# Row sums merged per head, squares as two bf16 terms, modulation as rows, and a first stage by half tiles in a hybrid attention and convolution layer on Trainium2

## The reference

```python
shift, scale, gate = jnp.split(mod, 3, axis=-1)          # mod = c @ w_ada + b_ada
u = layer_norm(x) * (1.0 + scale[:, None]) + shift[:, None]
proj = jnp.einsum('bsd,de->bse', u, w_in)
q, k, v, z_a, bg, cg, xin, z_c = jnp.split(proj, IN_SPLITS, axis=-1)
...
s = s + bias[None, :, None]                              # causal, T5 bias, 8 heads, 2 maps of 64
p = jax.nn.softmax(s, axis=-1)
a = p[:, :, 0] - lam * p[:, :, 1]                        # differential map, then a @ v
...
o = o * lax.rsqrt(jnp.mean(jnp.square(o), axis=-1, keepdims=True) + RMS_EPS)
y_attn = o * subln_gain * (1.0 - lambda_init) * jax.nn.silu(z_a)
y_conv = short_conv(bg, cg, xin, conv_w) * jax.nn.silu(z_c)
merged = g_a * (y_attn @ w_branch[0]) + g_c * (y_conv @ w_branch[1])
out = jnp.einsum('bsd,de->bse', merged, w_out)
return layer_norm(DEEPNORM_ALPHA * x + (1.0 + gate[:, None]) * out, ln_gain, ln_bias)
```

## Time and profile before

| | us |
|---|---|
| median of 3 runs (lowest, highest) | 3925.77 (3921.51, 4459.56) |
| the profiled execution, all cores | 3949.52 |
| span of its slowest core (core 1) | 3948.0 |
| spans of the cores | 3879.9 to 3948.0 |
| mean granted TensorE clock of the cores | 0.974 to 0.984 |

### The profile page before, as it was taken

One profiled execution on the slowest core, in us unless ns is written; L12 is line 12 of the kernel. 1 busy time (PEld: TensorE's weight loads), 2 busy tenths in 40 slices (PEclk: granted clock), 3 DMA queues, 4 the chain that ended last, 5 costly groups with the idle time before them and its releaser, 6 DMA issues.

```text
span 3948.0 us, 69802 instructions; the slowest of 8 cores (3879.9 to 3948.0 us)
## 1 busy us (share of the span) xinstructions
PE 3688.0 (93%) x18936; PEld 1530.1 (39%) x18936; DVE 2546.2 (64%) x4871; ACT 2491.7 (63%) x2902; POOL 178.2 (5%) x229
## 2 busy tenths in 40 slices
PE   7598889999998999999999999999999999999994
PEld 6334444343343343434333344333333433333332
DVE  1445656677666855678565876568657758758655
ACT  1244646677676676677676767667766766666671
POOL 0000000000000000000000000000000000000000
PEclk9899999999999999999999999999999999999997
DMA  6878977789799765576555655646456456456541
GB/s 171 228 220 172 206 180 173 143 223 209 148 222 219 188 149 136 134 176 170 132 137 129 187 126 125 138 133 178 123 132 168 124 133 173 126 132 167 129 109 51
DMA packets 413510, 623.39 MB, mean 158 GB/s; under 512 B 143531, under 2 KB 177451, under 8 KB 409676
## 3 DMA queue, kind: packets, MB, share of 16 engines
q1 hardware_dynamic: 413132, 618.92, 63.8%
HBM read 515.09 MB, written 103.67 MB: 157 GB/s over the span
## 4 chain that ended last, share of the span: by engine, by line
PE 78%; DMA 11%; issue 3%; ACT 3%; DVE 3%; SPq 2%; POOL 0%; ACTq 0%; DVEq 0%; POOLq 0%
PE ps L29 77%; ACT PB L43 2%; DMA TH<-s_scr 2%; DMA kT_scr<-KS 2%; SPq L160 2%; DMA ST<-wpk 2%; DMA q_scr<-QB 1%; DMA TH<-rho_scr 1%; DMA v_scr<-VS 1%; DMA rho_scr<-HS 1%; DMA s_scr<-HS 1%; PE ps L33 1%; DVE QS L48 0%; DMA m_scr<-BIG 0%; DVE PB L48 0%
## 5 line engine op out<-in xcount | busy, mean ns | idle before, releaser
L43 ACT ACTIVATE PB<-ps 128x1024 bf16<-128x1024 f32 (+1 forms) x2112 | 2017.9, 1009 | 764.5 <-PE ps L29 686.3
L29 PE MATMUL ps<-PB,V 128*128 128x512 bf16 (+6 forms) x4608 | 1242.4, 364 | 67.7 <-ACT PB L43 40.1
L29 PE MATMUL ps<-BIG,W 128*128 128x512 bf16 x4800 | 1231.9, 382 | 26.8 <-DVE BIG L48 12.5
L48 DVE TENSOR_TENSOR QS<-PB 128x1024 bf16<-128x1024 bf16 x896 | 617.4, 689 | 530.6 <-ACT PB L43 520.4
L29 PEld LDWEIGHTS ps<-BIG,W 128*128 128x128 bf16 x4800 | 465.7, 99 | 586.0 <-issue 60.5
L29 PE MATMUL ps<-Q,K 64*128 64x512 bf16 (+6 forms) x4608 | 653.0, 363 | 15.5 <-ACT PB L43 15.0
L29 PEld LDWEIGHTS ps<-PB,V 128*128 128x128 bf16 x4608 | 366.6, 99 | 741.2 <-issue 587.6
L48 DVE TENSOR_TENSOR QS<-QS 128x1024 bf16<-128x1024 bf16 x672 | 462.6, 688 | 33.0 <-DVE QS L48 1.4
L29 PE MATMUL ps<-UT,W 128*128 128x512 bf16 x1344 | 343.5, 385 | 6.9 <-DVE QB L53 2.0
L29 PEld LDWEIGHTS ps<-Q,K 64*128 64x128 bf16 x4608 | 145.5, 94 | 476.5 <-issue 462.1
L29 PE MATMUL ps<-W,UT 128*128 128x512 bf16 x896 | 228.3, 386 | 3.5 <-DVE KS L62 2.4
(11 more groups left out here) (96 smaller groups left out, 2153.8 us busy)
## 6 DMA issues: line engine op xcount, KB each, us to landing
W<-w_bf SPq DMA_DIRECT2D x704, 256.0 KB, 3.7
V<-v_scr SPq DMA_DIRECT2D x288, 256.0 KB, 5.2
K<-kT_scr SPq DMA_DIRECT2D x288, 256.0 KB, 5.4
ST<-wpk SPq DMA_DIRECT2D x104, 512.0 KB, 6.9
X<-x_all SPq DMA_DIRECT2D x64, 512.0 KB, 7.4
w_bf<-W SPq DMA_DIRECT2D x104, 256.0 KB, 8.8
v_scr<-VS SPq DMA_DIRECT2D x256, 64.0 KB, 5.3
kT_scr<-KS SPq DMA_DIRECT2D x64, 256.0 KB, 6.5
```

The lines of the kernel that those rows point to most:

```text
L29: return lambda e: e.matmul(out(), lhsT(), rhs(), start=start, stop=stop)
L43: return e.activation(out(), in_(), func, **kw)
L48: return lambda e: e.tensor_tensor(out(), in0(), in1(), op)
```

## The change

- **Row sums.** The `QS` tiles of a head's chunks are added up on DVE like a binary counter, the sum is added into the first tile of the diagonal chunk, and a head has two `onesAB` matmuls whatever j is. `QS` has 7 buffers instead of 9.
- **Squares.** The square is written as a bf16 tile (ACT), the f32 square (DVE) minus it as a second bf16 tile (DVE); eight one-column bf16 matmuls sum both.
- **Modulation.** `ada` is one call: the conditioning column is stationary, the f32 weights move (32 matmuls of 512 columns), four rows are evicted and turned into columns by 16 small matmuls. `masks` comes first on TensorE.
- **Start.** Tiles 0 and 1 are transposed and projected to V in half tiles; the staging pools are widened with buffers not yet in use (x blocks in `PB` and `QS`, V in `ON` and `QB`, K in the layer norm rows, Q in `vh`, head outputs in `TA`). K, V and Q units are loaded as f32 twice and written to `w_bf` at their second use, in tile 2. The mask spread is 8 transfers instead of 4, with the same rows. Constants are loaded later.
- **Output.** The adaLN gate is multiplied into the bf16 output weights once, and a DVE multiply for each 512 columns of output goes away.
- **Planning.** The planner's latencies and durations are shortened; tiles 0 and 1 get no convolution or merge work; 5 early items in place of 8.

```diff
@@ -191,10 +191,10 @@
 
 
 def simulate(g, nunits=200):
-    LAT = 0.2
+    LAT = 0.14
     DLAT = 4.5
-    CLAT = 6.5
-    BW = 220e3
+    CLAT = 5.5
+    BW = 240e3
     owner, lastvb = {}, {}
     freed = {}
...
@@ -267,13 +267,13 @@
                 d += 0.095
                 st["mode"] = md
             free[e] = t + d
-            o.end = t + d + 0.1
+            o.end = t + d - 0.03
...
-            free[e] = t + d
+            free[e] = t + max(0.05, d - (0.1 if e == "act" else 0.084 if e == "dve" else 0.0))
             o.end = t + d
         hpush(evs, (o.end + LAT, o.seq, 1))
...
+        PX0 = Pool("X0", list(PX.units) + [(("PB", i), ("PB", i + 1)) for i in (0, 2, 4, 6)] +
+                   [(("QS", i), ("QS", i + 1)) for i in (0, 2, 4)],
+                   list(PX.aps) + [PBT[:, i:i + 2].rearrange("p a b c -> p (a b c)").bitcast(F32)
+                                   for i in (0, 2, 4, 6)] +
+                   [QST[:, i:i + 2].rearrange("p a b c -> p (a b c)").bitcast(F32) for i in (0, 2, 4)])
+        PVS0 = Pool("VS0", list(PVS.units) + list(PON.units) + list(PQS_.units),
+                    list(PVS.aps) + list(PON.aps) + list(PQS_.aps))
+        PKS0 = Pool("KS0", list(PKS.units) + [(("LG", i),) for i in range(4)],
+                    list(PKS.aps) + [LGT[:, i].bitcast(BF16).rearrange("p (t o s) -> p t o s", t=8, o=2)
+                                     for i in range(4)])
...
-        def ada(part):
-            banks = [VB(PSE) for _ in range(8)]
-            for kp in range(4):
+        def ada():
+            rows_ = [pse() for _ in range(4)]
+            for k in range(8):
                 w = bigvb()
...
+                def wv(n, w=w):
+                    return lambda: w.ap().rearrange("p a b -> p (a b)").bitcast(F32)[:, n * 512:(n + 1) * 512]
+                g.dma((lambda w=w: w.ap().rearrange("p a b -> p (a b)").bitcast(F32)), A(w_ss[k]), writes=[(w, 0)],
+                      prio=1, nbytes=1 << 20)
+                for n in range(4):
+                    g.op("pe", 0.9, MM((lambda vb=rows_[n]: bank[vb.ap()][0:1, :]), A(ccol[:, k:k + 1]), wv(n),
+                                       start=(k == 0), stop=(k == 7)), [(w, 0), ("ccol", 0)], [(rows_[n], 0)],
+                         kind="F")
+            cvb = pse()
+            for n in (2, 3, 0, 1):
+                rw = VB(PTH)
+                fevac((lambda rw=rw: rw.ap()[0:1, :]), (lambda vb=rows_[n]: bank[vb.ap()][0:1, :]), [(rows_[n], 0)],
+                      [(rw, 0)])
+                fns = [MM((lambda b=4 * n + i_: bank[cvb.ap()][:, b:b + 1]),
+                          (lambda rw=rw, i_=i_: rw.ap()[0:1, i_ * 128:(i_ + 1) * 128]), A(one_f[:])) for i_ in range(4)]
+                g.op("pe", 1.0, fns, [(rw, 0), ("one_f", 0)], [(cvb, 0)], kind="F")
+            g.op("dve", 0.15, TT(A(modc[:]), (lambda: bank[cvb.ap()][:, 0:16]), A(bac[:]), ALU.add),
+                 [(cvb, 0), ("bac", 0)], [("modc", c_) for c_ in range(16)], 0)
+            g.op("dve", 0.1, TS(A(scale1[:]), A(modc[:, 8:16]), 1.0, None, ALU.add),
+                 [("modc", 8)], [("scale1", b) for b in range(8)], 0)
...
         def wunit(name):
             u = UID[name]
             w = VB(PW)
-            if u not in seen:
-                seen.add(u)
+            uses[u] = n = uses.get(u, 0) + 1
+            first = 2 if name[0] in ("k", "v", "q") else 1
+            if n <= first:
                 s_ = VB(PST)
-                g.dma(s_.ap, A(wpk[u]), writes=[(s_, 0)], prio=2, nbytes=1 << 19)
-
-                flex((0.98, 0.70), ACTV(w.ap, s_.ap, AF.Copy), CP(w.ap, s_.ap), [(s_, 0)], [(w, 0)], 4)
-                g.dma(A(w_bf[u]), w.ap, reads=[(w, 0)], writes=[("wbf", u)], prio=4, nbytes=1 << 18)
+                g.dma(s_.ap, A(wpk[u]), reads=[("modc", 13)], writes=[(s_, 0)], prio=2, nbytes=1 << 19)
+
+                if name[0] == "wo":
+                    def v2(f):
+                        return lambda: f().rearrange("p (k c) -> p k c", k=2)
+                    gs = G1h[:, name[1] * 512:(name[1] + 1) * 512]
+                    g.op("dve", 1.25, TT(v2(w.ap), v2(s_.ap), A(gs.unsqueeze(1).broadcast_to([128, 2, 512])), ALU.mult),
+                         [(s_, 0), ("G1h", name[1])], [(w, 0)], 4)
+                else:
+                    flex((0.98, 0.70), ACTV(w.ap, s_.ap, AF.Copy), CP(w.ap, s_.ap), [(s_, 0)], [(w, 0)], 4)
+                if n == first:
+                    g.dma(A(w_bf[u]), w.ap, reads=[(w, 0)], writes=[("wbf", u)], prio=4, nbytes=1 << 18)
             else:
                 g.dma(w.ap, A(w_bf[u]), reads=[("wbf", u)], writes=[(w, 0)], prio=2, nbytes=1 << 18)
...
@@ -920,7 +959,13 @@
                                 elif si == 7:
                                     acc_add(stk[1], stk.pop())
                                     acc_add(stk[0], stk.pop())
-                                    sums.append(stk[0])
+                                    sums.append((0, stk[0]))
+                                    while len(sums) > 1 and (sums[-1][0] == sums[-2][0] or c == j - 1):
+                                        lv_, a_ = sums.pop()
+                                        acc_add(sums[-1][1], a_)
+                                        sums[-1] = (max(lv_, sums[-1][0]) + 1, sums[-1][1])
+                        elif si == 0 and sums:
+                            acc_add(pb, sums[0][1])
...
                     if c == j:
-                        sums.append(pbs[0])
+                        sums = [pbs[0]]
...
-            flex((0.6, 0.69), ACTV((lambda: oe.ap()[:, 1, :]), (lambda: oe.ap()[:, 0, :]), AF.Square),
-                 TT((lambda: oe.ap()[:, 1, :]), (lambda: oe.ap()[:, 0, :]), (lambda: oe.ap()[:, 0, :]), ALU.mult),
-                 [(oe, 0)], [(oe, 1)], 4)
+            sq = VB(PTH)
+
+            def hl(i_):
+                return lambda: sq.ap().bitcast(BF16)[:, i_ * 512:(i_ + 1) * 512]
+            g.op("act", 0.6, ACTV(hl(0), (lambda: oe.ap()[:, 0, :]), AF.Square), [(oe, 0)], [(sq, 0)], 4)
+            g.op("dve", 0.69, TT((lambda: oe.ap()[:, 1, :]), (lambda: oe.ap()[:, 0, :]), (lambda: oe.ap()[:, 0, :]),
+                                 ALU.mult), [(oe, 0)], [(oe, 1)], 4)
+            g.op("dve", 0.69, TT(hl(1), (lambda: oe.ap()[:, 1, :]), hl(0), ALU.subtract), [(oe, 1), (sq, 0)],
+                 [(sq, 1)], 4)
             sv = VB(PSF)
             fns = [MM((lambda f=f: bank[sv.ap()][:, f:f + 1]),
-                      (lambda f=f: oe.ap()[:, 1, :].rearrange("p (q f) -> p q f", f=4)[:, :, f]),
-                      A(ones_f[:, 0:1])) for f in range(4)]
-            g.op("pe", 0.86, fns, [(oe, 1), ("ones_f", 0)], [(sv, 0)], kind="SQ", prio=1)
+                      (lambda f=f, i_=i_: hl(i_)().rearrange("p (q f) -> p q f", f=4)[:, :, f]),
+                      A(ones_b[:, 0:1]), start=(i_ == 0), stop=(i_ == 1)) for f in range(4) for i_ in range(2)]
+            g.op("pe", 0.5, fns, [(sq, 0), (sq, 1), ("ones_b", 0)], [(sv, 0)], kind="SQ", prio=1)
...
                         return rr.ap()[:, cs]
-                    g.op("dve", 0.7, TT(rv, bf(vb), A(G1h[:, cs]), ALU.mult), [(vb, 0), ("G1h", hc)], [(rr, hc)], 2)
-                    g.op("dve", 0.75, STT(rv, (lambda cs=cs: xo.ap()[:, cs]), ALPHA, rv, ALU.mult, ALU.add),
-                         [(xo, 0)], [(rr, hc)], 4)
+                    g.op("dve", 0.75, STT(rv, (lambda cs=cs: xo.ap()[:, cs]), ALPHA, bf(vb), ALU.mult, ALU.add),
+                         [(xo, 0), (vb, 0)], [(rr, hc)], 2)
                     g.op("dve", 0.665, (lambda e, hc=hc, rv=rv: e.bn_stats(sm.ap()[:, hc * 6:(hc + 1) * 6], rv())),
...
@@ -1338,8 +1398,10 @@
 
 
         nslots = [8 * (8 * j + 5) for j in range(NT)]
-        kvq = [(16 * 0.24 + 40 * 1.724) if 0 < j < NT - 1 else 0.0 for j in range(NT)]
-        ab_total = NT * 80 * 1.75 - 24 * 1.75
+        kvq = [(16 * 0.24 + 40 * 1.724) if 1 < j < NT - 1 else 0.0 for j in range(NT)]
+        nslots[0] = nslots[1] = 0
...
@@ -1350,20 +1412,19 @@
         budget = [max(0.0, r * n_ - k_) for n_, k_ in zip(nslots, kvq)]
 
         SEQ["wide"] = True
-        ada(1)
-        ada(0)
         masks()
+        ada()
         ln_tile(0)
-        t_groups(0)
         ln_tile(1)
         lam()
         vw = [v_weights(0), v_weights(1)]
-        v_group(0, vw[0], 0)
-        v_group(1, vw[1], 0)
-        t_groups(1)
-        v_group(0, vw[0], 1)
-        SEQ["wide"] = False
-        v_group(1, vw[1], 1)
+        for j in range(2):
+            if j == 1:
+                SEQ["wide"] = False
+            for hf in range(2):
+                t_groups(j, (hf,))
+                for hc in range(2):
+                    v_group(hc, vw[hc], j, (2 * hf, 2 * hf + 1))
         g0 = g.filtime
         for m in range(8):
```

168 lines of the change are left out of this document (88 added, 80 removed).

## The result

| | before | after |
|---|---|---|
| median (lowest, highest), us | 3934.0 (3921.5, 4459.6) | 3775.9 (3754.1, 3790.9) |
| the profiled execution | 3949.5 | 3780.95 |
| TensorE, VectorE, ScalarE busy, us | 3688, 2546, 2492 | 3535, 2681, 2514 |
| first score matmul, by core | 245.3 to 257.5 | 207.5 to 228.6 |

The ratio is 0.959, with a 95% interval of [0.952, 0.966]. On the profiled executions 168.6 us were gained of the 215 predicted, so 46 us are missing there; by the ratio it is 161 us of 214.

A forecast was written before the change was run, and what follows sets the result against it. TensorE's instructions were taken to bound the middle, dependency chains the start and end. 97 + 80 + 46 + 32 - 40 = 215 us off 3949.5, scaled to the median, gave 3712 us, range 3640 to 3815.

The forecast's parts named there:

- Row sums, 97 us: Heads' row sums: 448 onesAB matmuls go at 0.2175 us each, 97 us saved; VectorE's added adds cost nothing.
- Squares, 80 us: Each head's sum of squares: eight bf16 matmuls in 0.5 us replace four f32 ones of 1.75 us, 80 us saved.
- The halo row: Profile row of small bf16 halo matmuls, 62 ns each, used to price the bf16 matmuls of the squares.
- Start, 46 us: Up to the first score matmul: it moves from 248.6 to 206 us with 52 more matmuls done, 46 us saved.
- the gate's row: Profile row of the gate's f32 matmuls, 0.47 us a record, pricing the modulation at 30 us; 56 was taken instead.
- End, 32 us: Behind the last row sums: 2.5 us longer but holding 144 more matmuls, and fillers no longer run out before; 32 us saved.
- Given back, 40 us: Losses: 15 us for the stage reloading f32 K, V and Q in tile 2, 25 us for waits, 40 us together.
- the 100 that I had named as a sign of being wrong: Sign of a wrong prediction: TensorE's waits for exp tiles, or for the tiles of the squares, above 100 us.
- VectorE as a general brake: Rival: VectorE or ScalarE holds TensorE back through exp tiles, waits of 150 us instead of 25, 3837 us; chance 0.10.
- The f32 price of the squares: Rival: the squares' small bf16 matmuls cost what the f32 ones did, so nothing is saved there, 3792 us; chance 0.07.
- The transfer-bound start with a dearer reload: Rival: transfers still bound the start (15 us saved, not 46), 70 us given back and not 40, 3773 us; chance 0.17.
- The slower rival: Rival: DRAM round trips arrive later than planned, stalling TensorE in all 64 heads, up to 4064 us; chance 0.04.

The follow-up runs named there:

- b_both_plan: The kernel before with merged row sums, bf16 squares and the planner's new constants, its start, reload and end kept: ratio 0.973, 106 us less than before.
- a_oldstart: The changed kernel with the old start (modulation as columns ahead of the masks, tiles 0 and 1 whole, old staging): ratio 0.964 to before, -142 us.
- a_ne8: The changed kernel with eight early items of the last tile ahead of the last heads instead of five: 3776 us, 19 slower than the change.
- a_first1: The changed kernel with K, V and Q weights written back at first use, without the second f32 reading: mean 3718 us, 39 faster than the change.
- b_adds: The kernel before with VectorE's 224 added adds and all 576 onesAB matmuls kept: span 3950 us against 3948 for before.
- a_oldplan: The changed kernel with the planner's old constants (later DRAM round trips, full operation lengths): 3758 us against 3757 for the change.
- a_again: The changed kernel unedited, run again as yardstick on chip B: ratio 0.956 to before, mean 3757 us.
- a_late: The changed kernel with K, V, Q weights written back at first use and fillers of tiles 2 and 3 moved later: 3736 us, 3739 without the move.

## Why the prediction was right, and where it was not

**Row sums, 97 us.** The count (128 matmuls) and the cover on VectorE hold (2 us for the adds; VectorE is busy 2681 us, where 2736 were predicted). The price of 0.2175 us is not confirmed: alone the edit brought 48 us, and the fillers that run out ahead of the close explain, by the estimate, 21 of the 49 that are short. In the whole change they don't run out; its last 120 us in front of the close are busy 118:

```profile
3579.00:3619.00 40.00, 38.69 (x208) 14.40 (x204) 31.99 (x64) 27.57 (x31) 0.67 (x3) 1.00 0.57 138
3619.00:3659.00 40.00, 39.88 (x206) 14.16 (x203) 29.66 (x47) 30.29 (x35) 1.01 (x1) 1.00 0.53 132
3659.00:3699.00 40.00, 39.60 (x206) 15.99 (x205) 20.51 (x41) 25.19 (x32) 0.00 (x0) 1.00 0.33 89
```

That does not show the full term in it. In `b_both_plan` fillers last as well, and both terms with the planner brought 106 us, where 97 + 80 less the 25 us for waits are 152. With the 84 us that the squares brought alone, 22 are left for the row sums and the planner together.

**Squares, 80 us.** Shown: 84. The halo row was dearer than what it stood for: 62 ns, and measured are 34 (41 to 44 where scores or V follow). By that price it would be 90 to 95 us.

**Start, 46 us.** Predicted: modulation ready at 81 us, first score matmul at 206. Seen: V's first matmul waits until 84.7 us, and the first score matmul is at 207.5 to 212.1 us on the four cores whose clock stood at 0.97 or 0.98. Two errors of sizes cancelled, which is luck: the 64 records took 32.6 us and not 56 (the gate's row, 30, was the right one), but TensorE waited 18.2 us for `w_ss` between them; I had written that transfers don't bound this. On cores at 0.79 to 0.82 the same point is at 221 to 228.6 us. The time of the whole kernel did not follow the score matmul: `a_oldstart` gives 18 to 32 us for the start, not 46.

**End, 32 us.** `a_ne8` gives 19 to 30 for half of the moved work, which does not contradict 32 for all of it; the multiply that went was not measured alone.

**Given back, 40 us.** The idle time from 250 to 3650 us grew by 40.4 us. I had split it 15 and 25 between the reload and the waits; `a_first1` shows 39 for the reload alone, so 15 was too small. That the sum of 40 was right is not shown: `b_both_plan`, without the reload, has the same idle time (171.4 us), and two cores of before differ by 37 us in it. TensorE's waits for exp tiles rose from 66 us (49.8 + 16.3, core 1 of before, 250 to 3780 us) to 104 (66.9 from ScalarE, 36.9 from VectorE, core 4, 250 to 3650 us), which is more than my 25 and just over the 100 that I had named as a sign of being wrong.

**What is missing, 46 us.** Set in parts by the ratios: both terms and the planner brought 106 us (`b_both_plan`) where the sum had 152, so 46 less; everything else, start, end, output and reload, brought 55 (0.973 to 0.959) where the sum had 46 + 32 - 15 = 63. Each ratio is known to 27 us or so, but the larger part of what is missing lies in a kernel that has the old start. Its cause is open.

My own candidate was the granted clock, of which no step of the sum had anything. Core 4 and core 2 of the changed kernel's execution carry the same instructions (18328 and 18336 matmul records), at 0.964 and 0.980 of the clock, and are busy 3535.4 and 3481.9 us: 53.5 us. In the profiled execution of before, cores 1 and 5 (0.977 and 0.984) differ by 27.5 us, 3688.0 and 3660.4. By busy time the slowest core would have lost some 26 us to its clock beyond what before's had lost. By spans nothing is left: 3779.4 - 3717.6 = 62 us after, 3948.0 - 3879.9 = 68 us before. And in `a_first1` cores 4 and 5 stand at 0.81 from 150 to 250 us and at 0.84 to 0.86 up to 350, and end at 3716 and 3717 us, cores 2 and 3 with 0.95 or more at 3713 and 3714. So what the low clock costs is not shown.

That the parts come near the whole is luck in part. On chip A, `a_oldstart` (the change with the old start) is 36 us faster than `b_both_plan`, although it has the reload, 39 us on chip B, and the end is worth 19 to 30. The other 45 to 56 us come from parts that have no term in the sum, or next to none, and were never switched alone: the empty budgets of tiles 0 and 1, the other buffers, the later constants, the multiply of the output (3 us in the end's term).

**Rivals.** VectorE as a general brake (3837 us) is refuted by `b_adds` for the adds under the old plan; under the new one TensorE's waits for VectorE doubled (16.3 to 36.9 us), and `a_oldplan` shows that halving such a wait changes nothing. The f32 price of the squares is refuted. The transfer-bound start with a dearer reload (3773 us) came nearest in time, 3 us from the median, and half of it was true: the reload cost more than I gave it, while the start came as forecast where the clock was full. The slower rival's waits exist; what they cost is not shown (`a_oldplan`: 0), and it is not hundreds.

## What to carry to other kernels

- An instruction taken off the bounding engine is worth its time only while there is other work to take its place; look at the last hundred microseconds ahead of the close before multiplying count by price, and check that fillers last. That alone did not make up the loss here, so measure the edit by itself as well.
- When an edit saves work in a dense stage, ask which transfers it adds in the stretch where the DMA engines are at 0.8 or more: one line of reload policy was worth 39 us, a quarter of the whole change.
- Parts that were measured one by one have to be added up again: here they leave 45 to 56 us to edits that nobody had priced. And count in the trace what an edit moved before reading its time (`a_ne8`: half).
- A wait that disappears from the list is not time gained (`a_oldplan`: 24 us less in TensorE's list, 0 in the time).

## What the runs showed of the hardware

- TensorE's granted clock stood at 0.79 to 0.82 (262.5 ns for a 512-column matmul instead of 217) behind a start that was dense from 139 us on: on cores 4 and 5 from 150 to 450 us, on cores 0 and 1 from 150 to 350 us, on cores 6 and 7 at 0.97 to 0.98 up to 250 us and at 0.80 to 0.81 from 350 to 450 us, on cores 2 and 3 never. Pairs of cores entered and left it together. From 1400 to 3650 us, with TensorE busier still, it was 1.00 on all eight, and in the profiled execution of `a_again`, the same kernel, no core had it. What selects a pair, or an execution, is open.
- Two cores of one pair can end 116 us ahead of a third at nearly the same clock (0.985 against 0.981, `b_both_plan`), with a 256 KB load landing in 5.0 and not 8.1 us. In `a_late` cores 4 and 5 did so in one execution out of five (3603 and 3586 us against 3718 us and more) and ended at 3745 and 3744 us in another, so it is neither the core's data nor its place in the program.
- f32 matmuls of 512 columns with a one-column stationary operand took 0.51 us a record (32.6/64) on average: 0.33 us once they ran (6 in 2 us from 26 to 36 us), about 0.5 in the 6 us before that, and about 0.8 in the first 4 us behind the hole at 55 us, where the granted clock was 0.50. The masks' took 0.87 (13.99/16) all the way at a granted clock of 1.00. The number of stationary columns alone does not make that difference: the gate's, with 128 columns as well, took 0.44 at 313 us (7.03/16) on the same core. What does is open.
